# The input projection of a hybrid block: column tiles in pairs with seven products instead of eight

## The reference

```
h = RMSNorm(x)
[qA,kA,vA,zA, qB,kB,vB,zB, aB,bB, gate] = h @ W_in
yA = DiffAttn(qA,kA,vA) * silu(zA)
yB = RMSNorm(GatedDeltaNet(conv(qB,kB,vB), aB, bB)) * silu(zB)
m  = sigmoid(gate_A) * (yA @ W_upA) + sigmoid(gate_B) * (yB @ W_upB)
x  = x + m @ W_out
```

## Time and profile before

| | us |
|---|---|
| three runs | 940.66, 940.84, 944.18 |
| median | 940.84 |
| span of the profiled execution | 940.7 |
| busy: PE, DVE, ACT, POOL | 925.9, 605.4, 372.4, 291.9 |

### The profile page before, as it was taken

How to read it: one execution, slowest core, us unless ns; L and a number is a source line. 1 busy time by engine, 2 the same in 40 slices (tenths; PEclk the granted TensorE clock), 3 DMA queues, 4 the chain that set the end, 5 groups by cost and what they waited for, 6 DMA issues and landing times.

```text
span 940.7 us, 15067 instructions
## 1 busy us (share of the span) xinstructions
PE 925.9 (98%) x5251; PEld 765.3 (81%) x5251; DVE 605.4 (64%) x1406; ACT 372.4 (40%) x790; POOL 291.9 (31%) x225
## 2 busy tenths in 40 slices
PE   7999999999999999999999999999999999999898
PEld 6788888888788878888887888888888878888787
DVE  6777677647576766756726465476466567655993
ACT  5422332444333432433335455454555551123341
POOL 4222233353222222232233134133132133225552
PEclk9999999999999999999999999999999999999999
DMA  6112111222211211220111010111111114344403
GB/s 230 34 45 56 45 45 45 49 54 57 68 58 34 68 57 34 68 68 24 57 34 34 23 35 23 34 35 30 27 36 34 45 35 134 99 150 179 154 0 134
DMA packets 73000, 58.12 MB, mean 62 GB/s; under 512 B 4114, under 2 KB 62700, under 8 KB 72940
## 3 DMA queue, kind: packets, MB, share of 16 engines
q1 hardware_dynamic: 70700, 55.23, 19.9%
q10 hardware_dynamic: 2240, 2.12, 0.7%
HBM read 48.93 MB, written 8.40 MB: 61 GB/s over the span
## 4 chain that ended last, share of the span: by engine, by line
PE 91%; DVE 4%; POOL 2%; issue 1%; ACT 1%; DMA 1%; SPq 0%; DVEq 0%; ACTq 0%; POOLq 0%
PE PS L1344 21%; PE PS L1342 21%; PE PS L1346 21%; PE PS L1659 3%; PE PS L1684 3%; PE PS L1806 3%; PE PS L1805 3%; PE PS L1804 3%; PE PS L1677 2%; PE PS L1415 1%; POOL w_lo L718 1%; PE PS L1515 1%; PE PS L1508 1%; PE PS L1495 1%; PE PS L1529 1%
## 5 line engine op out<-in xcount | busy, mean ns | idle before, releaser
L1342 PE MATMUL PS<-h_hi,w_hi 128*128 128x512 f32 x784 | 312.0, 398 | 3.0 <-POOL w_lo L718 2.0
L1344 PE MATMUL PS<-h_lo,w_hi 128*128 128x512 f32 x784 | 314.8, 402 | 0.0
L1346 PE MATMUL PS<-h_hi,w_lo 128*128 128x512 f32 x784 | 313.5, 400 | 0.0
L718 POOL TENSOR_TENSOR w_lo<-w_raw,w_hi 128x512 fp32r<-128x512 f32 x100 | 148.2, 1483 | 434.2 <-ACT w_hi L871 433.2
L1342 PEld LDWEIGHTS PS<-h_hi,w_hi 128*128 128x128 f32 x784 | 147.5, 188 | 34.6 <-issue 2.4
L1344 PEld LDWEIGHTS PS<-h_lo,w_hi 128*128 128x128 f32 x784 | 147.5, 188 | 27.9 <-issue 0.7
L1346 PEld LDWEIGHTS PS<-h_hi,w_lo 128*128 128x128 f32 x784 | 147.7, 188 | 27.2 <-issue 0.8
L871 ACT ACTIVATE w_hi<-w_raw 128x512 fp32r<-128x512 f32 x100 | 62.7, 627 | 47.8 <-PE PS L1346 47.6
L2211 DVE TENSOR_REDUCE mx<-PS 128x1 f32<-128x1024 f32 (+7 forms) x64 | 48.3, 755 | 36.8 <-PE PS L1664 36.7
L1927 DVE SCALAR_TENSOR_TENSOR acc<-pre,cw,acc 128x1024 f32<-128x1024 f32 x36 | 56.2, 1562 | 1.3
L1143 ACT ACTIVATE prob<-PS,nm,r_qk 128x1024 f32<-128x1024 f32 (+7 forms) x64 | 52.6, 829 | 4.7 <-DVE nm L2215 4.5
(11 more groups left out here) (287 smaller groups left out, 1550.4 us busy)
## 6 DMA issues: line engine op xcount, KB each, us to landing
w_raw<-in_w_in SPq DMA_DIRECT2D x98, 256.0 KB, 2.9
x_in<-in_x SPq DMA_DIRECT2D x8, 512.0 KB, 7.8
zv<-gate_dram SPq DMA_DIRECT2D x8, 512.0 KB, 4.1
out_sb<-in_x SPq DMA_DIRECT2D x4, 1024.0 KB, 12.4
out<-out_sb SPq DMA_DIRECT2D x16, 256.0 KB, 2.1
gate_dram<-gate_st SPq DMA_DIRECT2D x7, 512.0 KB, 2.9
grow<-g_dram ACTq DMA_DIRECT2D x8, 256.0 KB, 3.2
w_raw<-in_w_up_gdn SPq DMA_DIRECT2D x8, 256.0 KB, 2.8
```

The costliest lines, as they stand in the source:

```text
L718: pool.tensor_tensor(lo[:, b, :], w_raw[:, b, :], hi[:, b, :].bitcast(F32), ALU.subtract)\
L1342: pe.matmul(dst, w, hi, start=first, stop=False)
L1344: pe.matmul(dst, w, lo, start=False, stop=False)
L1346: mm = pe.matmul(dst, lo_w, hi, start=False, stop=last)
```

## The change

The diff, cut:

```diff
+        G_AB, G_GATE, G_VA, G_FILL = 0, 1, 2, 6
+        B_FILL = [(GA, 5), (GA, 6), (GA, 7), (ZA, 0), (GB, 0), (GB, 1), (ZA, 1), (GB, 2), (ZA, 2), (GB, 3), (ZA, 3),
+                  (QK, 1, 0), (QK, 0, 0)]
+        C_FILL = [(QK, 1, 1), (QK, 0, 1), (QK, 1, 2), (QK, 0, 2), (QK, 1, 3), (QK, 0, 3), (GB, NK - 1), (GB, 4), (GB, 5), (GB, 6)]
+        B_TILES, C_TILES = len(B_FILL), len(C_FILL)
...
+        S_PAIRS = [(CONV, 0), (GATE, 1), (CONV, 2), (GATE, 3), (CONV, 4), (ZB, 0), (CONV, 6), (ZB, 2), (CONV, 8), (CONV, 10)]
+        S_ORDER = [(1, 2, 5, 6, 3, 4, 7)] * (N_PAIRS - 1) + [(4, 1, 2, 5, 6, 3, 7)]
...
-        B_FIRST, B_STEPS = 122, 90
-        B_AT = {"state": 0, "products": 5, "v_new": 8, "update": 14, "X": 52, "Y4": 57, "X4": 62, "V4": 66, "out": 66,
-                "Y5": 71, "V5": 76, "Y6": 81, "V6": 86}
+        B_FIRST, B_STEPS = 98, 65
+        B_AT = {"state": 0, "products": 4, "v_new": 6, "update": 10, "X": 36, "Y4": 40, "X4": 44, "V4": 47, "out": 47,
+                "Y5": 51, "V5": 54, "Y6": 58, "V6": 61}
...
-        C_STEPS = ({7: (2, 9, 11), 6: (2, 9, 11), 5: (2, 9, 11), 4: (2, 8, 13), 3: (2, 8, 14), 2: (3, 8, 12), 1: (3, 8, 11), 0: (3, 8, 16)},
-                   {7: (2, 9, 10), 6: (2, 9, 8), 5: (2, 9, 7), 4: (2, 8, 7), 3: (2, 7, 6), 2: (2, 6, 5), 1: (2, 5, 4), 0: (3, 4, 0)})
+        C_KT, C_KBACK, C_OUT = 48 * B_TILES - 40, (48 * B_TILES - 22, 48 * B_TILES - 17), 48 * B_TILES - 10
+        C_QT, C_S_FIRST, C_V_FIRST, C_FIRST = 3, 7, (10, 15), 22
+        C_STEPS = ({7: (1, 7, 7), 6: (1, 7, 6), 5: (1, 7, 6), 4: (1, 6, 7), 3: (1, 6, 8), 2: (1, 6, 8), 1: (2, 5, 7), 0: (2, 5, 9)},
+                   {7: (1, 7, 6), 6: (1, 7, 5), 5: (1, 7, 4), 4: (1, 6, 4), 3: (1, 5, 4), 2: (1, 5, 3), 1: (1, 4, 3), 0: (2, 3, 0)})
...
+        T_ORDER = (1, 2, 4, 3)
+        T_LO_DVE, T_LO_POOL = (1, 2, 3), (4,)
+        S_FORM = {1: "W11", 2: "W12", 3: "S4", 4: "W22", 5: "S1", 6: "S2", 7: "S3"}
...
+            def load_pair(p):
+                col = s_column(p)
+                for name, k, c in (("W11", 0, 0), ("W12", 4, 0), ("W22", 4, 1), ("W21", 0, 1)):
+                    if p == 0:
+                        if name in ("W11", "W12"):
+                            sp.wait_ge(w_lo_ready.sem, w_lo_ready.at(2 * G_GATE + ("W11", "W12").index(name)))
+                    else:
+                        reader = {"W11": 1, "W12": 3, "W22": 4, "W21": 7}[name]
+                        sp.wait_ge(f_lo.sem, f_lo.at(p - 1, s_place(p - 1, reader)))
+                        if name == "W11":
+                            sp.wait_ge(sum_ready.sem, sum_ready.at(p - 1, 3))
+                        elif name == "W22":
+                            sp.wait_ge(sum_ready.sem, sum_ready.at(p - 1, 1))
+                    sp.dma_start(S_RAWS[name].rearrange("p (k n) -> p k n", k=4), w_in_k[:, k:k + 4, col + c * P:col + (c + 1) * P])\
+                        .then_inc(slab_loaded[name].sem, 16)
+            def store_pair(p):
...
+            load_pair(0)
+            sp.wait_ge(h_lo_ready.sem, h_lo_ready.at(2 * NK - 1))
+            for n, part in enumerate((h_hi, h_lo)):
+                sp.dma_start(h12_dram[n * P:(n + 1) * P, :, :], part[:, 0:4, T1].bitcast(F32)).then_inc(h12_stored.sem, 16)
+                if p < N_PAIRS:
+                    load_pair(p)
...
+            sp.wait_ge(h12_stored.sem, h12_stored.at(0))
+            for n, part in enumerate((h_hi, h_lo)):
+                sp.dma_start(part[:, 0:4, T1].bitcast(F32), h12_dram[n * P:(n + 1) * P, :, :]).then_inc(h12_loaded.sem, 16)
+            last = N_PAIRS - 1
+            sp.wait_ge(f_lo.sem, f_lo.at(last))
+            sp.wait_ge(sum_ready.sem, sum_ready.at(last))
...
+            for k in range(4):
+                h_whole(F22, k)
+            split_lo(G_GATE, 1)
+            for k in range(4):
+                h_whole(F21, k)
+            def form_lo(q):
+                p, i = q // 7, q % 7
+                pool.wait_ge(f_hi.sem, f_hi.at(p, i + 1))
+                hi, lo = s_slot(q)
+                pool.tensor_tensor(lo, S_RAWS[S_FORM[S_ORDER[p][i]]], hi.bitcast(F32), ALU.subtract).then_inc(f_lo.sem, 1)
...
+                pool.tensor_tensor(lo, t_sum(n, k), hi.bitcast(F32), ALU.subtract).then_inc(t_lo_pool.sem, 1)
+            for q in range(4):
+                form_lo(q)
+            for k in range(4):
+                t_rest(4, k)
+            for q in range(4, 7 * N_PAIRS):
+                form_lo(q)
...
+            def form_hi(q):
+                if q >= 7 * N_PAIRS:
+                    return
+                p, i = q // 7, q % 7
+                name = S_FORM[S_ORDER[p][i]]
+                if name in slab_loaded:
+                    act.wait_ge(slab_loaded[name].sem, slab_loaded[name].at(p))
+                else:
+                    act.wait_ge(sum_ready.sem, sum_ready.at(p, S_SUMS.index(name) + 1))
+                if q >= SLOTS:
+                    before = q - SLOTS
+                    act.wait_ge(f_used.sem, f_used.at(before // 7, before % 7 + 1))
+                elif q < 2:
+                    act.wait_ge(w_used.sem, w_used.at(2 * G_GATE + q))
+                act.activation(s_slot(q)[0], S_RAWS[name], ACT.Copy).then_inc(f_hi.sem, 1)
...
+            def product_of(p, i):
...
+                if product == 6:
+                    pe.wait_ge(quarter_out.sem, quarter_out.at(p, 1))
+                elif product == 3:
+                    pe.wait_ge(tmp_ready.sem, tmp_ready.at(p, TMP_Y5))
+                elif product == 7:
+                    pe.wait_ge(quarter_out.sem, quarter_out.at(p, 2))
+                pe.wait_ge(f_lo.sem, f_lo.at(p, i + 1))
+                bank = s_banks(p)[{1: "X", 6: "X", 7: "X", 2: "Z", 5: "Y", 3: "Y", 4: "W"}[product]]
+                hi, lo = s_slot(7 * p + i)
+                for k in range(4):
+                    if p == 0 and product in (5, 6, 7, 4):
+                        n = {5: 1, 6: 2, 7: 3, 4: 4}[product]
+                        if n in T_LO_DVE:
+                            pe.wait_ge(t_lo_dve.sem, t_lo_dve.at(4 * T_LO_DVE.index(n) + k))
+                        else:
+                            pe.wait_ge(t_lo_pool.sem, t_lo_pool.at(k))
+                    cols = slice(k * P, (k + 1) * P)
+            for p in range(N_PAIRS):
...
+            def strassen_over():
+                pe.wait_ge(h12_loaded.sem, h12_loaded.at(0))
+                pe.wait_ge(quarter_out.sem, quarter_out.at(N_PAIRS - 1))
...
+            for k in range(4):
+                h_whole(F11, k)
+                h_whole(F12, k)
+                if k > 0:
+                    t_difference(1, k - 1)
+            t_difference(1, 3)
+            for k in range(4):
+                t_difference(2, k)
+                t_rest(1, k)
+            for name in S_SUMS[:3]:
+                weight_sum(0, name)
+            for k in range(4):
+                t_difference(4, k)
+                t_rest(2, k)
+            dve.wait_ge(ab_T.sem, 1)
+            dve.tensor_copy(ab[:, :, :].rearrange("p t c -> p (t c)"), PS[:, 6, 0:64]).then_inc(a2_dve.sem, 1)
+            for k in range(4):
+                t_difference(3, k)
+            weight_sum(0, "S4")
+            for k in range(4):
+                t_rest(3, k)
+            dve.wait_ge(pre_zero.sem, 2)
             dve.wait_ge(vec_ready.sem, 5)
-            with dve.Fori(0, 12) as c:
-                dve.wait_ge(conv_acc.sem, conv_acc.at(c - 1))
-                dve.tensor_copy(cw[:, :], half_conv_flat[:, bass.ds(c * TAPS, TAPS)]).then_inc(conv_w_ready.sem, 1)
-                dve.wait_ge(proj_out.sem, proj_out.at(c))
-                dve.wait_ge(conv_w_ready.sem, conv_w_ready.at(c))
-                dve.wait_ge(conv_done.sem, conv_done.at(c - 1))
-                for tap in range(TAPS):
-                    src = pre[:, tap:tap + SEQ]
-                    if tap == 0:
-                        ins = dve.tensor_scalar(acc[:, :], src, cw[:, 0:1], None, ALU.mult)
-                    else:
-                        dve.wait_ge(conv_acc.sem, conv_acc.at(c, tap))
-                        ins = dve.scalar_tensor_tensor(out=acc[:, :], in0=src, scalar=cw[:, tap:tap + 1], in1=acc[:, :],
-                                                       op0=ALU.mult, op1=ALU.add)
-                    ins.then_inc(conv_acc.sem, 1)
-                dve.wait_ge(conv_th.sem, conv_th.at(c))
-                dve.scalar_tensor_tensor(out=conv_flat[:, bass.ds(c * SEQ, SEQ)], in0=th[:, :], scalar=1.0, in1=acc[:, :],
-                                         op0=ALU.add, op1=ALU.mult).then_inc(conv_done.sem, 1)
+            for p in range(N_PAIRS + 1):
+                kind, m = S_PAIRS[p - 1] if p > 0 else (None, 0)
+                if p > 0:
+                    quarter(p - 1, 3)
+                    quarter(p - 1, 4)
+                if p == N_PAIRS:
+                    break
+                if kind == CONV:
+                    tap(m + 1, 0)
+                    conv_silu(m)
+                    tap(m + 1, 1)
```

(15 more changed lines are left out.)

560 lines of the change are left out of this document (424 added, 136 removed).

## The result

The changed kernel takes 1017.1 us (median of 4 runs, 1014.3 to 1018.9) against 941.4 for the kernel before: 1.080 times as long, 95% interval 1.078 to 1.083. The forecast was 988.5, with a range of 950 to 1008. The direction was right, the size was not, and the time lies outside the range. The profiled execution has a span of 1012.6 us, 71.9 more than that of before; what follows is about these two. (It is the quickest of the four, with a mean granted clock of 0.969; the others have 0.963 to 0.966.)

A forecast was written before the change was run, and what follows sets the result against it. PE bounds the kernel, busy 98% of the span, with DVE next. 940.7 - 27.2 saved + 27 start + 22 pairs + 6 boundary + 15 B + 3 C + 2 clock = 988.5 us, range 950 to 1008.

The forecast's parts named there:

- the clock: Behind PE's waits at the start and four transitions: half-speed matmuls, 1.1 us per wait of about 2.65; +2 us (0 to 6).
- B: Stage of steps with solve and Y4: with 36 matmuls of fill instead of 52, PE waits before Y4; +15 us.
- C: Stage of heads and probabilities: less fill hardly fits the room before the transposes, the last head waits; +3 us.
- The saving: PE's matmuls in pairs and tiles: 2232 instead of 2352, 120 fewer at 0.2267 us; -27.2 us.
- The start: Before product 6 of pair 0: PE waits for DVE's 40 new operations, slowed by 18 of POOL; +27 us.
- The pairs: Four conv-to-light pair transitions: PE waits 5 us each before product 7 for DVE, plus 2 in the last pair; +22 us.
- The boundary: Behind the last pair: DVE's quarters, taps and decay chain take 21 us against PE's 16 of work; +6 us.
- (a): Rival: POOL's touches fall into idle time, DVE has only its own work; 929.5 us, chance 0.11.
- (b): Rival: start as computed, pairs and B mostly covered by the light pairs' slack; 957 us, chance 0.2.
- (c): Rival: C and B have no room, each C step waits about 0.6 us, B's second half too; 1004 us, chance 0.12.

The follow-up runs named there:

- Experiments 4: Changed kernel with POOL's rests of stationary blocks, its quarters of h and T4's rests replaced by memsets of zero, which read nothing (computes less): 978.9 us.
- experiments 7: Changed kernel with the start reordered: slabs W22 and W21 loaded before W11 and W12, ACT taking the first tile out before rounding T1: 1016.9 us.
- experiment 5: Changed kernel with POOL's rests of the fill's weight slabs in stages B and C written as zeros (computes less): 992.3 us.
- experiment 6: Changed kernel without taps 1 to 3 of the last conv tile, 3.9 us of DVE (computes less): 1010.6 us.
- experiment 2: Changed kernel with PE filling its six longest waits before the delta net with small products of the identity: 1011.5 us.
- 11: Changed kernel with DVE's sums for the next head's q norms put ahead of a head's last prob_c, in C only: 1012.4 us.

## Why the prediction was right and wrong

The cause that I named, DVE's new operations and their turns with POOL, holds. What failed are sizes. The term for the clock was 2 us and measured 18.5. B was 15 and is 25.2, and C was 3 and is 12.1, both because waits were put at nothing (B's prologue, the scores at each turn of heads) and because of the clock. The restarts, 5 us, had no term.

**The saving** (-27.2) stands as a count; it can't be seen by itself.

**The start** (27): 29.1. The quarter was forecast to end at 79.4 and ended at 79.46, by steps of which three were off and cancelled; this is luck. DVE began at 36.6, not 34.4. I had 18 turns with POOL, 19.6 us; between 36 and 79 DVE's operations took some 11 us more than alone, the worth of ten turns. And I left out DVE's 6.6 us of idle time for slabs that SP holds back behind POOL's gate tile rests, a DMA queue that I didn't follow. Experiments 4 and 7 show how these hang together. The price of a turn (1.09) was right: 1.08 in the trace. The Trainium skill (SBUF — State Buffer, "Who interferes with whom") says that the second of the two blocks until the first is through; the rows of experiments 4 and 5 agree in kind, turn by turn. A POOL rest at 45.99 took 4.70 us, while DVE had operations back to back until 49.54: POOL can be the one that is held, and for more than one operation of DVE.

**The pairs** (22): 28.5. The four transitions came as forecast, 2.9 to 3.5 us of wait where I had 5, but before product 6, not product 7: quarter 1 is already late. With their half speed these pairs are 5.1 to 5.6 long by too much, 21.5 together. The rest is the last pair (4.5, of it two waits of 3.4), pair 6 (1.6, with a wait of 0.98) and 0.3 in each of the others.

**The boundary** (6): 8.5. The chain that I priced is not the one that PE waited for. The decay operations held ACT, and ACT held the bank of the vA tile; the step "who is queued behind the waiting instruction" was missing for ACT. It is shown for 4 us (experiment 6); the wait of 3.41 behind POOL's powers is read from rows only.

**B** (15): 25.2. The waits that I priced are there in their size: 1.2 to 1.7 in five steps, 3.2 and 3.3 in two, where I had 1.2 and 3.2. What failed is the prologue, whose wait of 3.24 I had not looked at, and the clock: 6.7 us lost, in three stretches of B. I had noted the differing chain lengths without asking for their cause; it was again POOL.

**C** (3): 12.1. I looked at the room before the transposes, which held, and not at the scores, which wait for the exponentials at each turn of heads (6.5 us with what follows, at three turns), nor at the last head beyond its two rows. (The fill of a head before is 185 matmuls, not 186, which changes nothing.)

**The clock** (2): 18.5. This is the term that was most mis-sized, and it was in my hands. The earlier trace rows gave the price of one wait, and my own sum had five waits over 2.65 us in it, seven with B's two of 3.2; 5 x 1.1 is 5.5 already, and I wrote 2. In the trace there are ten such stretches with work behind them, each 3.4 us or more at half speed and with 1.5 us or more lost. Two of them (window columns as in experiment 2):

```profile
148.20:151.60 3.40, 3.40 (x9) 2.66 (x9) 2.86 (x3) 0.00 (x0) 0.25 (x1) 0.51 0.37 100
44.00:49.00 5.00, 5.00 (x13) 3.84 (x13) 5.00 (x10) 3.56 (x7) 3.01 (x1) 0.50 0.00 2
```

9 matmuls in 3.40 us instead of 15; 13 in 5 instead of 22.

**The sum.** The waits alone were forecast at 73 and are 72.8. That is partly luck, since start and pairs were a little too dear and C far too cheap. Of the 24 us that were missing, 16.5 are the clock, 5 the restarts, and some 3 are not assigned. The rest of the program gained 4.1 us that I had not seen: the wait of 2.65 us at the product with W_out with its half speed is gone after; why it goes was not tried.

**The rivals.** (a), that POOL's touches fall into idle time, is refuted: the quarter came at 79, and with POOL writing only the kernel is 38 us faster. (b) is refuted by the four waits. (c), no room in B and C, was the nearest in time (1004), and was given a chance of 0.12; yet its mechanism was not what I wrote. B has nearly enough fill: with POOL's reads taken out (experiment 5) it is 5 us late instead of 25, and C still 7 instead of 12.

## What to carry to other kernels

Before moving operations to two engines that hold each other up when both read SBUF, as DVE and POOL do here, count the pairs that will overlap, also where one of them is tiny and on a chain; if the loss of a turn (1.08 us here) is more than the operation itself (0.6), do both on one engine. When a sum has waits of some us on the tensor engine, give each its half-speed stretch as a term of its own. And follow each late result through every queue behind it, ACT's and SP's too, before pricing it at its first reader.

## What the runs showed of the hardware

- A DVE operation of 128x28 elements (0.19 us) took 1.16 to 1.23 us when it met a POOL operation of 1.3 us that reads SBUF: the size of the DVE operation did not matter. A POOL memset in the same place did not hold it.
- A POOL rest of 1.28 us took 4.70 beside DVE operations that followed one another without a gap, and 1.7 to 1.8 beside ones that came in turns with it.
- Of eleven waits of PE of 2.7 us or more in the kernel after, nine went with a stretch of 3.4 us or more at a granted clock of 0.5, of which 3.0 us or more lay behind the wait (5.5 behind the wait of 10.9, in which the clock had fallen already). Two at the boundary, 2.79 and 3.41, were not, though waits of 2.76 and 2.26 at the same place in experiment 2 were; what tells them apart is open. Single waits of 2.0 and less in the other stages were not, but the clock fell 0.5 us behind one of 1.94 (830.26), with one of 1.68 close behind. The same wait can go either way: that of 2.0 in the last pair was followed by half speed in experiments 7 and 11 and not in the kernel after, and one of 3.37 in experiment 5 (193.4) was not. Filling the waits with small products kept the clock at 1.00 (experiment 2, up to 303 us).
